# Decays of the cached keys, from a stage of their own into the score steps of an attention kernel

## The chip, the cores and the metric

The program runs on one core of one Trainium2 chip. The metric is the device time of one execution in microseconds (us).

## What is computed

Two layers of a decoder are run for a prompt of 2048 rows and for a group of 8 samples of one new row each. The change lies in the second layer, forgetting attention with 16 heads of 64. A sample attends to 4096 cached keys (32 pages of 128 rows) and to its new row:

```
csum = cumsum(concat([past_logf, logf]))           # along the keys
s = q.k * ATTN_SCALE + cq[..., :, None] - ck[:, :, None, :]
p = softmax(where(mask, s, -inf));  out = p @ v_all
```

The decay of a cached key is thus the sum of the log-forget values of all keys behind it. It depends on `cache_logf`, the page table and the new row alone, and has the shape of one number for each sample, head and key.

## The kernel before

The program is a row of stages. Each stage has its own semaphores and ends in a barrier of all engines. Behind the projections of layer 1 (`project1`) come `past`, `attention` and `out1`.

`past` makes the decays, in two groups (NG = 2) of 4 samples x 32 pages = 128 pages, one page on a partition. SyncE loads the page numbers, GpSimd gathers the log-forget rows of the pages with two indirect DMAs (1 MB each), VectorE runs 16 scans per group, one per head, TensorE adds up the totals of later pages with a matmul, VectorE turns the sums round (two passes over 128x2048), and TensorE transposes 32 blocks of 128x128, which VectorE copies into `C.decay`.

`attention` handles the prompt in 640 score steps: 16 heads x 4 chunks of 512 queries x 4, 8, 12 or 16 blocks of 128 keys. The order of everything on every engine is a list, `SEQ`, that `schedule()` writes out; each engine walks through it in order. A step `QK` has two or three matmuls on TensorE, an exp on ScalarE and an add into `acc` on GpSimd (weights go through a ring of 8). With each step goes one `M`, a matmul whose row maxima serve a chunk up to 22 steps ahead: VectorE reads it with a `reduce_max`. `M`, `MR` and `LS` share two PSUM banks, so that `M` number k waits until VectorE has read number k-2. `PV` weighs the values of four blocks; it comes behind the steps n with n mod 4 = 1. `OF` (VectorE) finishes a chunk.

The decode of the 8 samples is laid between these steps, as work at the end of given steps. For a sample: `SD` (VectorE adds decay to the scores), `SM` (maximum), `SA` (TensorE turns it, and waits for `SM`), `SB`, `SC`, `SS`, `SE` (exp), `SL` (sums), `SX` (TensorE, waits for `SL`), `SR`; then `VG` 0 to 7 (TensorE, 4 pages of values each, through the two halves of the tile `vp`), `VN` (the new row), `VM` (VectorE masks the result, `at_cm`), `VA` (TensorE, one-column matmuls, waits for `VM`) and `VC`. Before, a sample takes 80 steps, from step 0 on.

## Time and profile before

| | us |
|---|---|
| median of 3 runs | 3209.83 (3197.79 to 3213.23) |
| the profiled execution, its own time | 3206.77 |
| span of the profile | 3205.2 |
| TensorE busy | 2845.1 (89%) |
| VectorE, ScalarE, GpSimd busy | 1596.3, 1024.8, 1380.8 |

Times in the profile are counted from the span's start. `past` and `attention` lie between about 1894 and 2960 us. "PE" is the matmul, "PEld" the weight load of TensorE, DVE is VectorE, ACT ScalarE, POOL GpSimd, SP SyncE. What stands behind "<-" in a line of a wait is who ended it.

### The profile page before, as it was taken

The numbers are of one execution on the slowest core, as the hardware profiler recorded it, in microseconds if no ns is written. First come the engines' busy times: TensorE is split into PE (matmuls) and PEld (weight loads), VectorE is DVE, ScalarE is ACT, GpSimd is POOL, SyncE is SP. The second block draws the span as 40 slices with busy tenths as digits, with TensorE's granted clock in tenths as the row PEclk, the third lists the DMA queues.
The fourth block names the chain that finished last, engine by engine and source line by source line (L and its number), as shares of the span: only waits on it lengthen the run. The fifth ranks groups of instructions, "written<-read, shape, count | busy, mean of one in ns | idle before, by whom it ended". The sixth has DMA issues, their size and how long they took to land. (4 is left out here: it accounts for less than half of the span.)

```text
span 3205.2 us, 46929 instructions
## 1 busy us (share of the span) xinstructions
PE 2845.1 (89%) x17133; PEld 2257.1 (70%) x17133; DVE 1596.3 (50%) x2148; ACT 1024.8 (32%) x1721; POOL 1380.8 (43%) x986
## 2 busy tenths in 40 slices
PE   3887979695998999879999957999999999999999
PEld 2887878683674999879999954555555555554787
DVE  4222223234365579888555545455455555553432
ACT  4323232322245222212112212444444444544100
POOL 0000000001000477666988845766766777777000
PEclk9998989897999999989999986999999999999899
DMA  4101010104563688879777748877977877874532
GB/s 122 35 21 40 20 40 20 40 13 148 173 181 121 195 265 287 259 248 314 250 250 247 256 147 191 248 202 204 245 204 221 237 206 234 228 213 133 179 118 74
DMA packets 327904, 547.51 MB, mean 171 GB/s; under 512 B 76093, under 2 KB 220129, under 8 KB 319212
## 3 DMA queue, kind: packets, MB, share of 16 engines
q1 hardware_dynamic: 263564, 471.12, 49.9%
q10 hardware_dynamic: 61120, 58.83, 5.3%
q0 software_dynamic: 3008, 14.81, 1.3%
q8 instruction: 124, 2.03, 0.3%
q14 instruction: 88, 0.72, 0.1%
HBM read 449.58 MB, written 95.12 MB: 170 GB/s over the span
## 5 line engine op out<-in xcount | busy, mean ns | idle before, releaser
L1151 POOL TENSOR_TENSOR p_kp<-p_kp,p_qb 128x1024 f32<-128x1024 f32 x256 | 628.6, 2483 | 385.1 <-DMA p_kp<-in_cache_k_dram 305.3
L1993 POOL TENSOR_TENSOR at_acc<-at_acc,at_w 128x512 f32<-128x512 f32 (+3 forms) x576 | 644.0, 1118 | 250.8 <-ACT at_w L2121 186.2
L2153 DVE TENSOR_REDUCE at_mx<-at_mx 128x1 f32<-128x512 f32 (+3 forms) x640 | 382.8, 608 | 447.3 <-PE at_mx L2028 322.3
L112 PE MATMUL p_pb<-p_w,x_xh 128*128 128x256 f32 x2048 | 593.5, 290 | 8.1 <-DVE p_w L1465 8.0
L113 PE MATMUL p_pb<-p_w,x_xh 128*128 128x256 f32 x2048 | 580.8, 284 | 0.0
L114 PE MATMUL p_pb<-p_w,x_xl 128*128 128x256 f32 x2048 | 580.5, 283 | 0.0
L2121 ACT ACTIVATE at_w<-at_st,c_nckt 128x512 f32<-128x512 f32 (+3 forms) x640 | 390.0, 622 | 382.6 <-PE at_st L2054 195.8
L1567 DVE TENSOR_REDUCE p_sc<-p_kp 128x16 f32<-128x1024 f32 x256 | 307.5, 1214 | 219.9 <-POOL p_kp L1151 219.8
L112 PEld LDWEIGHTS p_pb<-p_w,x_xh 128*128 128x128 f32 x2048 | 392.4, 192 | 20.0 <-issue 11.0
L113 PEld LDWEIGHTS p_pb<-p_w,x_xh 128*128 128x128 f32 x2048 | 393.9, 192 | 0.0
L114 PEld LDWEIGHTS p_pb<-p_w,x_xl 128*128 128x128 f32 x2048 | 393.0, 192 | 0.0
L112 PE MATMUL l_pb<-x_xh,l_wh 128*128 128x412 f32 x800 | 289.1, 361 | 73.4 <-DVE l_wl L857 73.4
L2069 PE MATMUL at_o<-at_w,at_v 128*64 128x512 f32 (+3 forms) x1280 | 292.8, 558 | 0.5 <-ACT at_w L2121 0.5
L113 PE MATMUL l_pb<-x_xl,l_wh 128*128 128x412 f32 x800 | 286.2, 358 | 0.0
L114 PE MATMUL l_pb<-x_xh,l_wl 128*128 128x412 f32 x800 | 285.7, 357 | 0.0
L2028 PE MATMUL at_mx<-at_km,at_q 65*128 65x512 f32 (+3 forms) x640 | 254.0, 400 | 17.4 <-POOL at_onesh L1968 12.1
L2052 PE MATMUL at_st<-at_q,at_k 128*128 128x512 f32 (+3 forms) x640 | 268.1, 419 | 0.8 <-ACT at_w L2121 0.8
L112 PE MATMUL o_pp<-o_wh,o_mh 128*128 128x512 f32 (+1 forms) x544 | 220.7, 406 | 35.0 <-DVE o_wl L586 22.4
L2054 PE MATMUL at_st<-at_q,at_k 65*128 65x512 f32 (+3 forms) x640 | 238.8, 373 | 0.0
L2052 PEld LDWEIGHTS at_st<-at_q,at_k 128*128 128x128 f32 x640 | 122.6, 192 | 137.7 <-issue 113.4
L113 PE MATMUL o_pp<-o_wl,o_mh 128*128 128x512 f32 (+1 forms) x544 | 215.9, 397 | 0.0
L114 PE MATMUL o_pp<-o_wh,o_ml 128*128 128x512 f32 (+1 forms) x544 | 215.4, 396 | 0.0
(293 smaller groups left out, 3840.4 us busy)
## 6 DMA issues: line engine op xcount, KB each, us to landing
p_kp<-in_cache_k_dram SPq DMA_DIRECT2D x256, 512.0 KB, 4.9
at_vp<-in_cache_v_dram SPq DMA_DIRECT2D x256, 512.0 KB, 5.4
o_mt<-mixed SPq DMA_DIRECT2D x32, 512.0 KB, 5.4
p_raw<-in_w_in_dram SPq DMA_DIRECT2D x32, 512.0 KB, 7.2
at_q<-qh SPq DMA_DIRECT2D x32, 512.0 KB, 10.8
at_k<-kh SPq DMA_DIRECT2D x32, 512.0 KB, 8.5
l_raw<-in_w_in_dram SPq DMA_DIRECT2D x20, 512.0 KB
mixed<-l_w POOLq DMA_DIRECT2D x8, 1028.0 KB, 4.2
```

The costliest lines, as they stand in the source:

```text
L112: nc.tensor.matmul(out, lhs[0], rhs[0], start=(k == 0), stop=False)
L113: nc.tensor.matmul(out, lhs[0], rhs[1], start=False, stop=False)
L114: return nc.tensor.matmul(out, lhs[1], rhs[0], start=False, stop=(k == nk - 1))
L1151: nc.gpsimd.tensor_tensor(kp[:, g % 4], kp[:, g % 4], qb[:], ALU.mult).then_inc(kmul, 1)
L1567: nc.vector.tensor_reduce(sc[:, b % 2].rearrange("p (h g) -> p h g", g=z.PG)[:, :, r], by_head(kp[:, g % 4], z.H), AX.X, ALU.add).then_inc ...
L1993: nc.gpsimd.tensor_tensor(t[:, 512 - wd:512], t[:, 512 - wd:512], W[n % RW][:, 0:wd], ALU.add).then_inc(accd, 1)
L2028: last = nc.tensor.matmul(MX[r % 2][:, 0:wd], Q2[s][0:HR, t * P:(t + 1) * P], KM[s][0:HR, seg * 512:seg * 512 + wd], start=True, stop=seg < c)
L2052: nc.tensor.matmul(ST[n % 2][:, 0:wd], K1[s][:, ks], Q1[s][:, q0:q0 + wd], start=True, stop=False)
L2054: last = nc.tensor.matmul(ST[n % 2][:, 0:wd], K2[s][:, ks], Q2[s][:, q0:q0 + wd], start=False, stop=not diagonal)
L2069: last = nc.tensor.matmul(O[u % 2][y:y + HD, 512 - wd:512], V[s][:, kb + x, :], W[(n + x) % RW][:, 0:wd], start=kb + x < 2, stop=kb + x >= ...
L2121: nc.scalar.activation(W[n % RW][:, 0:wd], ST[n % 2][:, 0:wd], ACT.Exp, bias=C.nckt[:, kb, u // NC:u // NC + 1]).then_inc(ex, 1)
L2153: nc.vector.reduce_max(mx[:, u % 2, j, seg:seg + 1], MX[r % 2][:, 0:wd], AX.X).then_inc(mread, 1)
```

## The change

`past` is gone as a stage. Its work is laid into `SEQ`: the scans four at a time (`PS`, behind steps 16, 19, ... 37), the totals (`PT`, `PL`, `PA`, up to step 42), the turning round as one pass (`PM`, steps 43 to 50), the transposes (`PP`, steps 45 to 52, four each), the copies (`PC`, steps 47 to 54) and the new row (`PN`, 54). Its two large tiles lie in `vp`, so the first pages of values are loaded from step 54 on and not at the start. The decode's sample b begins at step 62 + 72 b, and takes 72 steps instead of 80. On GpSimd the setup is put in another order; the eight `affine_select` of `headmask` become `HM` behind steps 34, 38, ... 62. Page numbers are loaded behind the first three of the eight loads of head 0, and the gathers are issued then.

```diff
-        at = [1 + x for x in range(len(tail) - VG - 4)] + [13 + 8 * r for r in range(VG)] + [71, 72, 74, 76]
-        span = N // B
+        at = [x for x in range(len(tail) - VG - 4)] + [11 + 8 * r for r in range(VG)] + [68, 69, 70, 71]
+        span, first = 72, 62
         side = {}
+        for n in range(NG):
+            for x in range(H // 4):
+                m = H // 4 * n + x
+                side.setdefault(16 + 3 * m, []).append(("PS", n, x))
+                side.setdefault(43 + m, []).append(("PM", n, x))
+                side.setdefault(45 + m, []).append(("PP", n, x))
+                side.setdefault(47 + m, []).append(("PC", n, x))
+            side.setdefault(17 + 3 * (H // 4) * (n + 1), []).append(("PT", n))
+            side.setdefault(42, []).append(("PL", n))
...
+        for x in range(8):
+            side.setdefault(34 + 4 * x, []).append(("HM", x))
         for b in range(B):
             for w, x in zip(tail, at):
-                side.setdefault(span * b + x, []).append((*w, b))
+                side.setdefault(first + span * b + x, []).append((*w, b))
...
-            for x in range(NLD):
+            for x in range(3):
                 head_load(0, x)
+            for n in range(NG):
+                sp.dma_start(idx[:, n:n + 1], a["page_table"][n * z.SB:(n + 1) * z.SB, :].rearrange("b g -> (b g)")
+                             .rearrange("(q o) -> q o", o=1)).then_inc(idx_in, 16)
+            for x in range(3, NLD):
+                head_load(0, x)
...
+                elif w[0] == "PP":
+                    _, n, x = w
+                    m = H // 4 * n + x
+                    pe.wait_ge(dv, m + 1)
+                    if m >= 2:
+                        pe.wait_ge(copied, m - 1)
+                    else:
+                        pe.wait_ge(tadd, NG)
+                    for g in range(4):
+                        last = nc.tensor.transpose(CV[:, m % 2, g * GP:(g + 1) * GP], cum[n][:, 4 * x + g, :], C.ident[0:GP, 0:GP])
+                    last.then_inc(turned, 1)
...
+                elif w[0] == "PS":
+                    _, n, x = w
+                    if x == 0:
+                        dve.wait_ge(pmade, 1)
+                        dve.wait_ge(logf_in, 16 * NG)
+                    lv = logf[n].rearrange("q (t h) -> q t h", h=H)
+                    for h in range(4 * x, 4 * x + 4):
+                        last = nc.vector.tensor_tensor_scan(cum[n][:, h, :], onesp[:], lv[:, :, h], 0.0, ALU.mult, ALU.add)
+                    last.then_inc(scand, 1)
...
+                elif w[0] == "PM":
+                    _, n, x = w
+                    dve.wait_ge(tadd, n + 1)
+                    dve.wait_ge(totd, NG)
+                    nc.vector.scalar_tensor_tensor(out=cum[n][:, 4 * x:4 * x + 4, :], in0=cum[n][:, 4 * x:4 * x + 4, :], scalar=-1.0,
+                                                   in1=tot[:, n, 4 * x:4 * x + 4].rearrange("q (h o) -> q h o", o=1).broadcast_to([GP, 4, P]),
+                                                   op0=ALU.mult, op1=ALU.add).then_inc(dv, 1)
+                elif w[0] == "PC":
+                    _, n, x = w
+                    m = H // 4 * n + x
+                    dve.wait_ge(turned, m + 1)
+                    nc.vector.tensor_copy(C.decay[:, n * z.SB:(n + 1) * z.SB, 4 * x:4 * x + 4, 0:PG].rearrange("p b h g -> p h b g"),
+                                          CV[:, m % 2, 0:4 * GP].rearrange("p (h b g) -> p h b g", h=4, g=PG)).then_inc(copied, 1)
```

Where it moves instructions, VectorE first, at steps 16 to 31, before. `at_mx` rows are reads of `M`, `at_og` rows are `OF`.

```order
L2153 TENSOR_REDUCE at_mx<-at_mx 128x1 x7
L2168 TENSOR_TENSOR at_og<-at_o,at_ot 64x512
L2171 TENSOR_TENSOR at_og<-at_og,at_sg 64x512
L2153 TENSOR_REDUCE at_mx<-at_mx 128x1
L2159 TENSOR_REDUCE at_mneg<-at_mx 128x4
L2153 TENSOR_REDUCE at_mx<-at_mx 128x1 x12
L2159 TENSOR_REDUCE at_mneg<-at_mx 128x4
```

And now; the rows with `at_onesp` are the scans of `PS` (the listing calls a scan SCALAR_TENSOR_TENSOR, and the tiles inside `vp` by that name).

```order
L2144 TENSOR_TENSOR at_og<-at_o,at_ot 64x512
L2147 TENSOR_TENSOR at_og<-at_og,at_sg 64x512
L2129 TENSOR_REDUCE at_mx<-at_mx 128x1
L2135 TENSOR_REDUCE at_mneg<-at_mx 128x4
L2129 TENSOR_REDUCE at_mx<-at_mx 128x1 x2
L2155 SCALAR_TENSOR_TENSOR at_vp<-at_onesp,at_vp 128x128 x4
L2129 TENSOR_REDUCE at_mx<-at_mx 128x1 x2
L2135 TENSOR_REDUCE at_mneg<-at_mx 128x4
L2129 TENSOR_REDUCE at_mx<-at_mx 128x1
L2155 SCALAR_TENSOR_TENSOR at_vp<-at_onesp,at_vp 128x128 x4
L2129 TENSOR_REDUCE at_mx<-at_mx 128x1 x3
L2155 SCALAR_TENSOR_TENSOR at_vp<-at_onesp,at_vp 128x128 x4
```

Four scans now stand behind every third read. Next TensorE, where the first sample's decode ends, before: the one-column matmuls of `VA` at the end of step 74.

```order
L2069 MATMUL at_o<-at_w,at_v 64x512 x4
L2052 MATMUL at_st<-at_q_1,at_k_1 128x512
L2054 MATMUL at_st<-at_q_1,at_k_1 128x512
L2028 MATMUL at_mx<-at_km,at_q_0 128x512
L2108 MATMUL at_cv<-c_onescol,at_cm 128x1 x8
L2052 MATMUL at_st<-at_q_1,at_k_1 128x512
```

And now, steps 130 to 132 (`VN`, then `VM` on VectorE behind step 131, then `VA` behind step 132).

```order
L2076 MATMUL at_cv<-at_vp,at_sw 32x512 x2
L2008 MATMUL at_st<-at_q_1,at_k_1 128x128
L2010 MATMUL at_st<-at_q_1,at_k_1 128x128
L2012 MATMUL at_st<-at_identr,at_maskr 128x128
L1983 MATMUL at_mx<-at_km,at_q_1 128x512
L2008 MATMUL at_st<-at_q_1,at_k_1 128x512
L2010 MATMUL at_st<-at_q_1,at_k_1 128x512
L1983 MATMUL at_mx<-at_km,at_q_1 128x512
L2083 MATMUL at_cv<-c_onescol,at_cm 128x1 x8
```

The `PV` (`at_o`) that stood between `VM` and `VA` is not there any more. Last, TensorE at steps 46 to 48 now, with the transposes of `PP` (`at_cv<-c_ident,at_vp`); before, none of them stood in this stage.

```order
L2050 MATMUL at_cv<-c_ident,at_vp 128x128 x4
L2008 MATMUL at_st<-at_q_1,at_k_1 128x512
L2010 MATMUL at_st<-at_q_1,at_k_1 128x512
L1983 MATMUL at_mx<-at_km,at_q_1 128x512
L2050 MATMUL at_cv<-c_ident,at_vp 128x128 x4
L2008 MATMUL at_st<-at_q_1,at_k_1 128x512
L2010 MATMUL at_st<-at_q_1,at_k_1 128x512
L2012 MATMUL at_st<-at_identr,at_maskr 128x128
```

Each group of four follows a single score step, and waits for a copy that VectorE makes behind its read of that step's `M`.

## Rows read from the trace of the kernel before

**Rows 1.** The profile's page: busy time, share of the span, instructions.
```profile
PE 2845.1 (89%) x17133; PEld 2257.1 (70%) x17133; DVE 1596.3 (50%) x2148; ACT 1024.8 (32%) x1721; POOL 1380.8 (43%) x986
```
**Rows 2.** Seven windows of 80 steps: us; PE, PEld, DVE, ACT, POOL busy; clock; DMA.
```profile
2351.30:2480.30 129.00, 125.86 (x666) 71.80 (x665) 67.42 (x118) 60.10 (x100) 88.69 (x82) 0.95 0.79 214
...
2727.70:2850.50 122.80, 119.64 (x666) 68.82 (x665) 67.28 (x118) 60.10 (x100) 88.98 (x82) 1.00 0.79 224
sum 877.86, PE 856.18 PEld 491.13 DVE 471.76 ACT 420.68 POOL 620.87; mean PE 122.31 PEld 70.16 DVE 67.39 ACT 60.10 POOL 88.69
```
**Rows 3.** Timelines of SP, DVE, PE around `past`: start, duration, what, idle before.
```profile
1894.55 0.83 SPq L1592 DMA_DIRECT2D pa_idx<-in_page_table_dram  x2
1932.55 0.50 SPq L1857 DMA_DIRECT2D at_q<-qh  x1
...
1906.15 5.15 DVE L1639 TENSOR_TENSOR_SCAN pa_cum<-pa_ones,pa_l 128x128 f32<-128x128 f32 x16 [26.59 <-DMA pa_l<-in_cache_logf_dram,pa_idx]
1924.83 1.28 DVE L1657 COPY c_decay<-pa_pt 128x512 f32<-128x512 f32 x2
...
1942.77 0.47 PE L2028 MATMUL at_mx<-at_km,at_q 65*128 65x128 f32 x1 [12.10 <-POOL at_onesh L1968]
1954.69 0.77 PE L2052 MATMUL at_st<-at_q,at_k 128*128 128x512 f32 x1
```
**Rows 4.** Tile `at_k`, window 1930 to 1960: the last load of head 0.
```profile
L1857 SPq DMA_DIRECT2D at_k<-kl x1: 623/623/623, 1936.7 to 1936.7; - x1
...
DMA to landing us min/median/max: 8.8/10.7/16.0
```
**Rows 5.** Windows: head 0's loads; then the gathers of `past`.
```profile
1934.00:1950.00 16.00, 5.73 (x18) 3.89 (x18) 4.81 (x11) 0.58 (x1) 15.25 (x19) 0.50 1.02 219
1899.50:1905.50 6.00, 0.00 (x0) 0.00 (x0) 0.00 (x0) 0.00 (x0) 0.10 (x1) 0.50 0.82 330
```
**Rows 6.** Timelines of PE and PEld: two `M`, `PV` and the next `M`, transposes, `VA`.
```profile
2012.17 0.40 PE L2028 MATMUL at_mx<-at_km,at_q 65*128 65x512 f32 x1
...
2012.87 0.39 PE L2028 MATMUL at_mx<-at_km,at_q 65*128 65x512 f32 x1
...
2203.13 1.94 PE L2069 MATMUL at_o<-at_w,at_v 128*64 128x512 f32 x8
...
2205.57 0.40 PE L2028 MATMUL at_mx<-at_km,at_q 65*128 65x512 f32 x1
...
1880.00 0.46 PEld L1241 LDWEIGHTS p_tp<-c_ident,p_rows 128*128 128x128 f32 x4
...
2205.57 1.99 PEld L2108 LDWEIGHTS at_cv<-c_onescol,at_cm 128*128 128x128 f32 x16
```
**Rows 7.** Timeline of DVE: the read of the `M` issued at 2205.57.
```profile
2206.00 0.69 DVE L2153 TENSOR_REDUCE at_mx<-at_mx 128x1 f32<-128x512 f32 x1 [1.44 <-PE at_mx L2028]
```
**Rows 8.** Waits, 1972 to 2960: who waited for whom, us, times, longest.
```profile
PEld at_cv L2087 <- DVE at_l L2196: 10.3, 7, 1.5
PEld at_cv L2081 <- DVE at_smx L2182: 8.0, 7, 1.2
```
**Rows 9.** Groups of DVE, 1972.64 to 2960: busy us, mean ns, idle before.
```profile
L2205 DVE SCALAR_TENSOR_TENSOR at_cm<-at_cv,at_rl,at_headmask 128x1024 f32<-128x1024 f32 x8 | 10.2, 1276 | 7.5 <-PE at_cv L2101 7.5
...
L2178 DVE TENSOR_TENSOR at_sd<-at_sc,c_decay 128x512 f32<-128x512 f32 x7 | 8.5, 1210 | 0.0
```
**Rows 10.** Timelines of DVE and POOL at two places where both read SBUF.
```profile
1991.10 0.95 DVE L2171 TENSOR_TENSOR at_og<-at_og,at_sg 64x512 f32<-64x512 f32 x1
1991.65 1.54 POOL L1993 TENSOR_TENSOR at_acc<-at_acc,at_w 128x512 f32<-128x512 f32 x1
...
1960.04 0.71 DVE L2179 TENSOR_TENSOR at_sd<-at_sn,c_decay 128x16 f32<-128x16 f32 x1
1959.83 0.88 POOL L1993 TENSOR_TENSOR at_acc<-at_acc,at_w 128x256 f32<-128x256 f32 x1 [0.26 <-ACT at_w L2121]
```
**Rows 11.** Line L2179 (ns min/median/max), and L1993 by form (busy us, mean ns).
```profile
L2179 DVE TENSOR_TENSOR at_sd<-at_sn,c_decay x8: 175/179/712, 1960.0 to 2843.6; 128x16 f32<-128x16 f32 x8
...
L1993 POOL TENSOR_TENSOR at_acc<-at_acc,at_w 128x512 f32<-128x512 f32 x383 | 502.6, 1312 | 186.8 <-ACT at_w L2121 143.8 <-POOL at_acc L1993 1.3 <-POOL at_acc L1990 0.4
```

More of the change, by code:

```diff
@@ L1680, in attention @@
     VG = PG // 4
+    NG = B // z.SB
+    GP = z.GP
+    assert GP == P and NG * H * P * 2 <= 8 * z.D
     RW = 8
@@ L1812, in attention @@
         vp = S.sb("vp", [P, 2, 4, z.D])
+        flat = vp[:].rearrange("p s g d -> p (s g d)")
+        logf = [flat[:, P * H * n:P * H * (n + 1)] for n in range(NG)]
+        cum = [flat[:, P * H * (NG + n):P * H * (NG + n + 1)].rearrange("q (h t) -> q h t", t=P) for n in range(NG)]
+        idx = S.sb("idx", [GP, NG], I32)
+        onesp = S.sb("onesp", [GP, P])
+        tot = S.sb("tot", [GP, NG, H])
+        beyond = S.sb("beyond", [GP, GP])
+        lnew = S.sb("lnew", [1, B * H])
         sc = S.sb("sc", [P, H * PG])
@@ L1922, in _ @@
                     scores(w[-1] + 1)
+                elif w[0] == "PN":
+                    sp.wait_ge(turned, NG * H // 4)
+                    value_group(0, 0)
+                    value_group(0, 1)
                 elif w[0] == "VG":
@@ L1952, in _ @@
         def _(pool):
-            for s in range(2):
-                nc.gpsimd.memset(K2[s][HD:HR].bitcast(F32), 1.0).then_inc(made, 1)
-                nc.gpsimd.memset(Q2[s][HD:HR].bitcast(F32), 1.0).then_inc(onesd, 1)
+            nc.gpsimd.memset(maskf[:], 0.0).then_inc(masked, 1)
+            pool.wait_ge(masked, 1)
+            nc.gpsimd.affine_select(out=maskf[:], in_=maskf[:], compare_op=ALU.is_ge, fill=NEG, base=0,
+                                    pattern=[[-1, P]], channel_multiplier=1).then_inc(masked, 1)
+            nc.gpsimd.memset(onesp[:], 1.0).then_inc(pmade, 1)
+            nc.gpsimd.memset(beyond[:], 1.0).then_inc(pmade, 1)
+            nc.gpsimd.memset(C.decay[:, :, :, PG:PX], NEG).then_inc(pmade, 1)
+            pool.wait_ge(pmade, 3)
+            nc.gpsimd.affine_select(out=beyond[:], in_=beyond[:], compare_op=ALU.is_gt, fill=0.0, base=0,
+                                    pattern=[[-1, GP]], channel_multiplier=1).then_inc(pmade, 1)
+            pool.wait_ge(pmade, 4)
+            lv = beyond[:].rearrange("q (b g) -> q b g", g=PG)
+            nc.gpsimd.affine_select(out=lv, in_=lv, compare_op=ALU.is_ge, fill=0.0, base=PG - 1,
+                                    pattern=[[PG, z.SB], [0, PG]], channel_multiplier=-1).then_inc(pmade, 1)
+            pool.wait_ge(pmade, 5)
+            nc.gpsimd.memset(Q2[0][HD:HR].bitcast(F32), 1.0).then_inc(onesd, 1)
+            nc.gpsimd.memset(K2[0][HD:HR].bitcast(F32), 1.0).then_inc(made, 1)
+            pool.wait_ge(made, 1)
+            pool.wait_ge(onesd, 1)
+            pool.wait_ge(idx_in, 16 * NG)
+            for n in range(NG):
+                pool.indirect_dma_start(out=logf[n], out_offset=None, in_=a["cache_logf"].rearrange("n p h -> n (p h)"),
+                                        in_offset=bass.IndirectOffsetOnAxis(ap=idx[:, n:n + 1].bitcast(U32), axis=0)).then_inc(logf_in, 16)
+            nc.gpsimd.memset(Q2[1][HD:HR].bitcast(F32), 1.0).then_inc(onesd, 1)
+            nc.gpsimd.memset(K2[1][HD:HR].bitcast(F32), 1.0).then_inc(made, 1)
             pool.wait_ge(made, 2)
@@ L2074, in _ @@
                     pe.wait_ge(accd, HB * (h + 1))
+                    pe.wait_ge(made, 3)
                     ring_free(r)
@@ L2445, in hybrid_step @@
             C.decay = S.sb("decay", [P, z.B, z.H, z.PX])
-            past(nc, z, a, C, out)
             attention(nc, z, a, C, D, out)
```

149 lines of the change are left out of this document (44 added, 105 removed).

## The prediction

> **What bounds the kernel now.** First the page: TensorE is busy 89% of the span, no other engine above half [rows 1]. Then windows over the attention stage: of 122.80 us that a sample's 80 steps take at best, TensorE is busy 119.64, GpSimd 88.98, VectorE 67.28 [rows 2]. So in this stage the order on TensorE is the time. A microsecond of TensorE's work or waiting is a microsecond of the kernel; work of VectorE is free as long as TensorE does not come to wait for it. The same windows show a second thing. The seven sum to 877.86 us, which is 18.3 more than 7 x 122.80, and the longest (129.00) has a mean granted clock of 0.95, against 1.00 in the best [rows 2]: the low level (1.2 GHz instead of 2.4) costs 1 to 6 us a sample. Third the timelines around `past`. Its first DMA is issued at 1894.55, attention's first at 1932.55, TensorE does nearly nothing between; attention's first matmul is at 1942.77 and its first score step at 1954.69 [rows 3].
>
> **The change, part by part.**
>
> The stage goes: 1932.55 - 1894.55 = **-38.0** [rows 3]. The logf gather's latency (VectorE stood 26.59 us before its first scan) lies in these 38.
>
> The start of attention gets the gathers. Before, the first score step came 22.1 us after the first issue. The last load of head 0 was issued at 1936.7 and landed 16.0 later, at 1952.7, so 20.2 after the first [rows 4]; the loads ran at 219 GB/s with the DMA engines full (share 1.02) [rows 5]. The two gathers (2.1 MB) took some 6 us at share 0.82 in an empty machine [rows 5], so 4.9 us of all engines. They now fall between those loads and push the last landing to about 25.1, and with its semaphore the first score step to some 25.6: **+3.5**. Bounds: -2 (loads untouched, 20.2), +6.
>
> TensorE gets 32 transposes and two pairs of small matmuls. Four transposes at the full clock took 0.43 (1880.00 to the next load; the row has 0.46) [rows 6], eight groups 3.6, the matmuls some 0.7: **+4.3**. Bounds 3 and 7 (low clock).
>
> `PP` waits. From the issue of an `M` (2205.57) to the read of it (2206.00) pass 0.43 us [rows 6, 7]; the read takes 0.6 net of overlap (0.69 in its row), the copy `PC` 0.6 (two in 1.28) [rows 3], the semaphore 0.1: 1.7 to 1.8. TensorE has 0.23 of that filled (two `M` of neighbouring steps with both score matmuls between are 0.70 apart, three matmuls of 0.23) [rows 6]. `PP` number m waits for the copy m-2 behind the read of its own step, so it waits 1.5 us wherever no `PV` lies between: steps 47, 48, 50, 51, 52. **+7.5**. Queued behind it: the next score step, so ScalarE and GpSimd too. Bounds 2 and 10.
>
> `PS`. Alone a scan is 0.32 (16 in 5.15) [rows 3], four are 1.3. With three reads of 0.6 VectorE would need 3.1 us in three steps. TensorE takes 4 x 0.70 for four steps and 1.9 for their `PV` (2203.13 to the next `M` at 2205.57, less that step's own 0.5) [rows 6], so 3.5 for three: hidden. But not beside GpSimd. A multiply with two inputs in SBUF took 0.95 as GpSimd was adding, and GpSimd's next add 1.54 [rows 10] against a mean of 1.31 [rows 11]; a tiny operation with both inputs in SBUF, of 0.18 as a rule, took 0.71 and ended with the add beside it (1960.76 and 1960.71) [rows 10, 11]. The scans have both inputs in SBUF, GpSimd's adds of 512 columns take 1.3 each [rows 11], and one comes with each step, in stretches where steps without `PV` are 0.70 apart [rows 6]. So each scan can meet an add. If none does: 0. If each of the four waits a whole add: 3.1 + 4 x 1.3 = 8.3 us for three steps instead of 3.5, x8 = +38. I take half the adds met, 5.6 for 3.5, x8 = 17, less 2 for the groups in narrow steps: **+15**. The two banks that `M` shares carry the delay to TensorE.
>
> The Trainium skill (SBUF — State Buffer, Who interferes with whom) says that a VectorE instruction with two SBUF inputs and a GpSimd instruction that reads SBUF lock each other out for a whole instruction. That speaks for the upper end, where each scan waits out an add; the trace's 0.71 for 0.18 agrees with it, and only shows it for one operation at a time.
>
> The decode's new positions modulo 4. A `PV` (n mod 4 = 1) gives VectorE 1.9 us to catch up. `SA` waited 8.0 us in 7 samples, `SX` 10.3 in 7 [rows 8], `VA` never. Now `SD` (1.21 mean [rows 9], plus 0.18) stands behind a step without `PV`, and `SM` and `SA` behind the next two: 0.43 + 0.6 + 1.4 + 0.6 + 0.7 from the `M` of the first = 3.75, of which TensorE fills 1.6; the wait goes from 1.15 to 2.2, +1.1 x 8 = 9. `SX` gets a `PV` between it and `SL`: -10 x 8/7, about -11, but in three samples an `OF` (1.6) falls before `SL`, +4. `VM` takes 1.28 [rows 9] and `VA` follows one step later with no `PV` between: 0.43 + 0.6 + 1.28 + 0.1 - 0.9 = 1.5, x8 = 12. Net **+14**. Bounds 0 and 22. Queued behind `VA` are all score steps.
>
> The clock. `VA` is 16 weight loads with one-column matmuls, 1.99 us [rows 6], in which the array does next to nothing; the 18.3 us lost to the low level [rows 2] lie right behind it. Now it has 1.5 us of standing still ahead of it, and 2.2 more four steps later. I take the low level behind each of the eight at 3.7 us: 30 - 18 = **+12**. Bounds 0 and 22.
>
> Small: VectorE is freed of the first sample's decode while two `M` a step are read, -2; the low clock in the `PP` steps, +3. Setup on GpSimd, `HM` (8 x 1.04, the ring of 8 weights hides it), the tail (last `VC` behind step 637 instead of 636), the value pages (first used at step 73, loaded from 54): 0. Were the cover of `HM` gone it would cost 8.
>
> Sum: -38.0 + 3.5 + 4.3 + 7.5 + 15 + 14 + 12 + 1 = +19.3, on the profiled execution's own 3206.77: 3226. That execution lies 3.1 under the median, the measured runs spread by 15. **3227.**
>
> **Rivals.**
>
> (a) The cover holds; **3189**. The stage's 38 us come back nearly whole: scans meet few adds, the clock behaves as before. -38 + 3.5 + 4.3 + 5 + 3 + 4 + 0 = -18. For it: VectorE is busy only 67.28 of 122.80 us [rows 2]. Against it: the waits in rows 8, which stand there at 55% busy.
>
> (b) Halves cancel; **3210**. The waits of `PS` and of the positions come out at half. -38 + 3.5 + 4.3 + 6 + 8 + 10 + 7 = +1. For it: the bounds of three terms begin at 0.
>
> (c) The lock decides; **3248**. Each scan waits for a whole add, +38 instead of +15. It is slower than (the forecast) from about 2 us a scan on. For it rows 10; against it, that GpSimd runs out of adds when TensorE is held up.
>
> That the stage's work is not removed but only overlaps is sure from the order; the pages of values arriving late (72 steps instead of 80) I give next to nothing: pages still come 8 steps apart and 16 ahead, and the busiest windows have a DMA share of 0.79 [rows 2].
>
> **How the numbers follow.** Forecast (slower by some 0.5 to 0.9%) 0.42, (c) 0.10, (b) 0.30, (a) 0.18. A measurement of this kernel tells about 0.5% (16 us) from no change. The forecast's own range is 3218 to 3240; since it begins at the edge of 0.5%, a part of it (0.07) counts as no change. Slower 0.45, same 0.36, faster 0.19. For 8 in 10 the range takes in (b), most of (a) and most of (c): 3184 to 3246.
>
> **What would show it.** In the profile after: the first score step 25 to 26 us after attention's first DMA issue (right: start). Scans with a median above 0.6 us and TensorE waiting for VectorE's reads of `at_mx` by 10 us or more between steps 16 and 40 (right: `PS`; with scans near 0.4, (a)). TensorE waiting on `c_decay`'s copies about 1.5 us, five times. Waits on `at_cm` of 1.5 us, eight times, and on `at_smx` of 2.2; those on `at_l` mostly gone. Granted clock 0.93 to 0.96 over the samples' windows of 72 steps, with a low stretch behind each `VA`. The prediction is wrong if the scans slip between the adds, or if the clock stays high past `VA`; then it is (a) or (b).

## The result, and the profile after

The changed kernel took 3261.15 us (median of 4 runs, 3258.00 to 3266.26) against 3204.07 for the one before (3197.79 to 3213.23): ratio 1.0179, 95% interval 1.0153 to 1.0205, so +57 us. It is slower, as forecast, but by three times as much as the forecast's +19, and outside the range. In all that follows a ratio is that to the kernel before, run beside it on the same chip; 0.001 is 3.2 us.

Windows from the first exp of step 0 to that of step 80 and of step 639, so heads 0 and 1 and then the other fourteen (columns as in [rows 2]). First the kernel before:

```profile
1956.98:2090.93 133.95, 131.09 (x661) 76.44 (x661) 70.08 (x126) 59.45 (x97) 86.83 (x81) 0.90 0.87 236
2090.93:2958.02 867.09, 844.54 (x4611) 481.55 (x4610) 459.22 (x803) 419.08 (x690) 619.43 (x572) 0.98 0.76 213
```

The same windows after:

```profile
1916.80:2080.23 163.43, 135.13 (x567) 80.17 (x567) 108.72 (x177) 59.92 (x97) 95.66 (x88) 0.82 0.46 110
2080.23:3010.74 930.51, 889.39 (x4743) 495.31 (x4742) 467.83 (x805) 420.98 (x690) 624.66 (x573) 0.96 0.77 215
```

The score steps begin 40.2 us earlier (1916.80 for 1956.98), so the stage is gone as planned. Then they take 1093.9 us instead of 1001.0: +92.9. Of these, 29.5 lie in the first two heads, where the decays' work is and hardly any decode, and 63.4 in the other fourteen, where nothing of the decays is left. The two parts are not like for like: the kernel before has a whole sample's decode in its first two heads, and after all eight samples fall on the other fourteen (4743 matmuls there for 4611). The clock says how. With levels of 1.2 and 2.4 GHz, a mean clock c of full speed means that a share 2(1 - c) of the time ran at the low one: 163.4 x 0.36 + 930.5 x 0.08 = 133 us after, 134.0 x 0.20 + 867.1 x 0.04 = 61 before. TensorE spent some 70 us more at half speed (rounding leaves 20 on this), and each costs half a microsecond at most: about 35. The two traces' records of the clock, added up without rounding, have 137.8 us at the low level after (59.3 in the first two heads) and 53.7 before (26.4): 84 more, so the cost is at most 42.

The rest is waiting. The waits of TensorE's matmuls in the 640 steps (who for whom, us, times, longest), before:

```profile
PE at_mx L2038 <- DVE at_mx L2153: 10.2, 32, 0.9
PE at_cv L2081 <- DVE at_smx L2182: 5.9, 7, 0.9
PE at_mx L2028 <- DVE at_mx L2153: 4.1, 8, 0.6
PE at_cv L2087 <- DVE at_l L2196: 4.1, 7, 0.6
```

And after (TensorE's line numbers are 45 to 25 lower than before; L1983 is `M`, L2055 `SA`, L2062 `SX`, L2050 `PP`, L2083 `VA`):

```profile
PE at_mx L1983 <- DVE at_mx L2129: 18.8, 8, 4.6
PE at_cv L2055 <- DVE at_smx L2195: 14.9, 6, 3.3
...
PE at_cv L2062 <- DVE at_l L2209: 9.2, 7, 2.7
PE at_cv L2050 <- DVE c_decay L2177: 7.7, 5, 1.8
PE at_cv L2083 <- DVE at_cm L2218: 6.6, 8, 1.3
```

That is +14.7 at `M`, +9.0 at `SA`, +5.1 at `SX`, +7.7 at `PP`, +6.6 at `VA`: 43. With 6 for the added transposes (the busy time of their row) and up to 42 for the clock it makes up to 91 of the 93. TensorE's busy time says the same without the clock. It is the sum of the two windows of each kernel, before and after:

```profile
sum 1001.04, PE 975.63 PEld 557.99 DVE 529.30 ACT 478.53 POOL 706.25; mean PE 487.81 PEld 278.99 DVE 264.65 ACT 239.26 POOL 353.13
sum 1093.94, PE 1024.52 PEld 575.48 DVE 576.55 ACT 480.90 POOL 720.32; mean PE 512.26 PEld 287.74 DVE 288.27 ACT 240.45 POOL 360.16
```

TensorE stands still for 69.4 us instead of 25.4 (+44.0), and its work takes 1024.5 instead of 975.6 (+48.9), though only 38 more matmuls are counted. Waits of its weight loads are counted too further on; they begin earlier and so are longer (at `SA` 17.7 us for the matmuls' 14.9, at `SX` 11.8 for 9.2, at `VA` 9.2 for 6.6).

Where a wait and the clock meet is best seen at a sample's change-over. Timelines of TensorE, VectorE and GpSimd after, steps 131 to 137:

```profile
2161.46 0.39 PE L1983 MATMUL at_mx<-at_km,at_q 65*128 65x512 f32 x1
2163.13 2.96 PE L2083 MATMUL at_cv<-c_onescol,at_cm 128*128 128x1 f32 x16 [1.28 <-DVE at_cm L2218]
...
2167.52 2.82 PE L2025 MATMUL at_o<-at_w,at_v 128*64 128x512 f32 x8
...
2176.22 0.38 PE L2055 MATMUL at_cv<-c_ident,at_smx 128*16 128x128 f32 x1 [3.31 <-DVE at_smx L2195]
...
2172.04 1.75 DVE L2191 TENSOR_TENSOR at_sd<-at_sc,c_decay 128x512 f32<-128x512 f32 x1
2173.72 1.24 DVE L2192 TENSOR_TENSOR at_sd<-at_sn,c_decay 128x16 f32<-128x16 f32 x1
...
2171.97 4.35 POOL L1941 TENSOR_TENSOR at_acc<-at_acc,at_w 128x512 f32<-128x512 f32 x3 [2.74 <-ACT at_w L2096]
```

TensorE stands 1.28 us for `VM`, runs `VA` in 2.96 us (its weight loads in 2.88, for 1.99 in [rows 6]) and the `PV` behind it in 2.82 (1.94 in [rows 6]). Two steps on `SD` takes 1.75 + 1.24 us, beside three adds of GpSimd (experiment 13 tests that they are the reason), and `SA` is waited for 3.31 us; the score matmul behind that took 0.77 us where that of the step before took 0.51. Windows of the same stretch: the wait for `VM`, the first microsecond of `VA`, the rest of it with the `PV`, the steps up to `SA`'s wait, that wait, and what follows it (the last three columns are clock, DMA share and GB/s):

```profile
2161.85:2163.13 1.28, 0.00 (x0) 0.00 (x0) 1.28 (x3) 0.50 (x1) 0.61 (x1) 1.00 1.06 282
2163.13:2164.13 1.00, 1.00 (x8) 1.00 (x8) 0.55 (x1) 0.00 (x0) 0.00 (x0) 0.85 0.97 238
2164.13:2170.27 6.14, 6.14 (x22) 4.17 (x22) 0.64 (x2) 0.69 (x1) 1.26 (x1) 0.50 0.97 346
2170.27:2172.90 2.63, 2.63 (x10) 1.72 (x9) 1.46 (x2) 2.15 (x4) 0.93 (x1) 0.93 1.03 412
2172.90:2176.20 3.30, 0.01 (x1) 0.00 (x0) 3.30 (x5) 0.51 (x1) 3.01 (x3) 0.68 1.27 249
2176.20:2180.70 4.50, 4.48 (x13) 1.94 (x13) 3.24 (x7) 0.69 (x1) 1.39 (x2) 0.50 1.05 222
```

The clock is high over the wait for `VM`, falls inside `VA`, comes back, and falls again during the wait for `SA`. In the whole trace it falls within 4 us of the start of seven of the eight `VA` (before: four of eight), and a second time some 10 to 15 us behind the start of six of them. Windows of steps 120 to 128, 128 to 152 and 152 to 160 show that the loss is in this place alone (clock 1.00, 0.86, 1.00):

```profile
2140.56:2153.16 12.60, 12.29 (x75) 7.09 (x75) 6.51 (x12) 7.02 (x13) 8.68 (x10) 1.00 0.57 151
2153.16:2202.75 49.59, 44.26 (x210) 25.35 (x210) 27.06 (x47) 18.85 (x30) 26.62 (x25) 0.86 0.67 192
2202.75:2214.27 11.52, 11.52 (x63) 6.17 (x63) 4.52 (x8) 4.75 (x8) 9.48 (x9) 1.00 0.75 217
```

In the first head the scans do the same. VectorE, GpSimd and TensorE after, from step 15 on:

```profile
1944.34 5.63 DVE L2155 TENSOR_TENSOR_SCAN at_vp<-at_onesp,at_vp 128x128 f32<-128x128 f32 x4
...
1942.75 8.35 POOL L1941 TENSOR_TENSOR at_acc<-at_acc,at_w 128x512 f32<-128x512 f32 x6 [1.04 <-ACT at_w L2096]
...
1952.30 0.58 PE L1983 MATMUL at_mx<-at_km,at_q 65*128 65x256 f32 x1 [4.60 <-DVE at_mx L2129]
```

Four scans and the adds beside them take turns: 5.63 / 4 = 1.41 us a scan, 8.35 / 6 = 1.39 us an add. TensorE then stands 4.60 us. The next four scans took 1.36 us: TensorE had been held up, and GpSimd had no add until 1955.61. The eight groups took 5.63, 1.36, 1.90, 2.43, 5.54, 1.36, 5.33 and 1.36 us.

### The profile page after: what moved, and what is told of

Its sections match the earlier page's. It is cut to its first block and busy times, and to the rows that moved or that the text cites. A ratio compares the mean times of both kernels' runs of the same rounds, so it can differ in the third digit from the quotient of the medians.

```text
span 3258.8 us, 46976 instructions
## 1 busy us (share of the span) xinstructions
PE 2881.9 (88%) x17133; PEld 2262.4 (69%) x17133; DVE 1618.3 (50%) x2152; ACT 1027.2 (32%) x1721; POOL 1387.4 (43%) x986
## 5 line engine op out<-in xcount | busy, mean ns | idle before, releaser
L2025 PE MATMUL at_o<-at_w,at_v 128*64 128x512 f32 (+3 forms) x1280 | 314.1, 593 | 0.5 <-ACT at_w L2096 0.5
L1983 PE MATMUL at_mx<-at_km,at_q 65*128 65x512 f32 (+3 forms) x640 | 255.7, 402 | 33.4 <-DVE at_mx L2129 19.5
L2008 PE MATMUL at_st<-at_q,at_k 128*128 128x512 f32 (+3 forms) x640 | 275.8, 431 | 3.2 <-issue 2.4
```

What stands on the lines that cost most here:

```text
L1983: last = nc.tensor.matmul(MX[r % 2][:, 0:wd], Q2[s][0:HR, t * P:(t + 1) * P], KM[s][0:HR, seg * 512:seg * 512 + wd], start=True, stop=seg < c)
L2008: nc.tensor.matmul(ST[n % 2][:, 0:wd], K1[s][:, ks], Q1[s][:, q0:q0 + wd], start=True, stop=False)
L2025: last = nc.tensor.matmul(O[u % 2][y:y + HD, 512 - wd:512], V[s][:, kb + x, :], W[(n + x) % RW][:, 0:wd], start=kb + x < 2, stop=kb + x >= ...
```

## Experiments

Two theories stood against each other: A, the decode's new places are most of the loss; B, the work of the decays among the score steps is. The edits are to the changed kernel unless the text says otherwise, and the diffs show the lines that matter. The interval of a ratio is 0.002 to 0.004 to each side, so a difference between two experiments is known to some 9 to 16 us; where it is smaller than that, the traces have to carry the argument.

**1. The decode alone.** In the kernel before, with its stage:

```diff
-        at = [1 + x for x in range(len(tail) - VG - 4)] + [13 + 8 * r for r in range(VG)] + [71, 72, 74, 76]
-        span = N // B
+        at = [x for x in range(len(tail) - VG - 4)] + [11 + 8 * r for r in range(VG)] + [68, 69, 70, 71]
+        span, first = 72, 62
```

> The kernel before, its stage `past` kept, with only the decode's steps changed to those of the changed kernel (begin at 62, 72 a sample, same offsets). Theory A: the decode's new places are most of the loss. In the trace of after, heads 2 to 15, which hold nothing of the decays, take 930.5 us against 867.1 before, +63; so this kernel should be +50 to +65 us on before (3254 to 3269), with waits on at_smx and at_cm and a low stretch of the clock behind nearly each VA. Theory B: the work of the decays in steps 16 to 55 is most of it, and what heads 2 to 15 lose follows from it (a late start, a shifted GpSimd); then this one is +10 to +25 (3214 to 3229).

3259.48 us, ratio 1.0176 (1.0136 to 1.0216). The whole +57 is here, to within 15 us. Theory A holds, and the decays' work in the score steps costs about what the stage gave back, some 38 us. Its profiled execution was its slowest (3281.77 us; the others 3258.01 to 3264.40). Heads 0 and 1 in it, with neither decays nor a decode, and the rest:

```profile
1969.19:2090.96 121.77, 116.38 (x529) 71.51 (x529) 72.15 (x124) 59.48 (x97) 86.29 (x80) 0.89 0.55 131
2090.96:3031.35 940.39, 894.19 (x4743) 497.02 (x4742) 468.08 (x805) 420.94 (x690) 624.85 (x574) 0.95 0.77 213
```

Against this the decays' work made the first two heads 41.7 us longer (163.43), more than the 29.5 against the kernel before. Over all 640 steps the difference is 31.8 us (1093.94 for 1062.16), where the changed kernel's steps begin 40.2 us earlier than those of before. TensorE's matmuls wait in experiment 1 as they do after: 14.8 us at `SA`, 9.2 at `SX`, 6.6 at `VA`. Experiments 2 to 4 ran beside it.

**2. The chain spaced out.**

```diff
-        at = [x for x in range(len(tail) - VG - 4)] + [11 + 8 * r for r in range(VG)] + [68, 69, 70, 71]
+        at = [0, 0, 2, 2, 4, 4, 5, 6, 8, 8] + [11 + 8 * r for r in range(VG)] + [67, 68, 70, 71]
```

> The changed kernel with the chain of the decode's steps spaced: SD and SM at 0, SA and SB at 2, SC and SS at 4, SE 5, SL 6, SX and SR 8, VN 67, VM 68, VA 70, VC 71. Each piece of VectorE now has a PV or a second step between it and TensorE's next piece. Theory A (TensorE's waits at SA, SX and VA, and the low clock that follows a wait): waits on at_smx, at_l, at_cm fall from 17.7 + 11.8 + 9.2 us to under 10 together, the low stretches behind VA from about 17 to under 8, time -40 to -60 on after (3200 to 3220). Rival: the low clock follows the 16 one-column matmuls of VA itself, wait or not; then only the waits go, -20 to -30 (3231 to 3241), and the low stretches stay.

3249.34 us, ratio 1.0143 (1.0103 to 1.0184): -12, less than either forecast. The waits at `SX` went, those at `VA` fell to 2.2 us (matmuls), but those at `M` rose from 18.8 to 24.9, and those at `SA` stayed (12.3 us, five times, up to 2.8): `SD` and `SM` both stood at step 134 and `SA` two steps on, before the next `PV`.

**3. The scans' ones from PSUM.**

```diff
+                        nc.vector.tensor_copy(CV[0:GP, 1, 0:P], onesp[:]).then_inc(cvones, 1)
-                        last = nc.vector.tensor_tensor_scan(cum[n][:, h, :], onesp[:], lv[:, :, h], 0.0, ALU.mult, ALU.add)
+                        last = nc.vector.tensor_tensor_scan(cum[n][:, h, :], CV[0:GP, 1, 0:P], lv[:, :, h], 0.0, ALU.mult, ALU.add)
```

> The changed kernel with the ones that each scan multiplies by read from PSUM (the decode's buffer, free until step 42) instead of SBUF, so that a scan has one input in SBUF. Theory (the scans and GpSimd's adds hold each other up because both of a scan's inputs lie in SBUF): the scans' time, 393/415/1500 ns minimum, median, longest, loses its long ones (longest under 700), the two groups of four of 5.6 us fall to about 1.7, the waits of TensorE for the reads of at_mx in steps 16 to 40 shrink by some 8 us, and the time by 8 to 15 us with the clock (3246 to 3253). Rival (VectorE is late because of what it has to do, and a PSUM input is no faster): scans stay as they are or get slower, and the time stays within 4 us of after.

3240.36 us, ratio 1.0115 (1.0076 to 1.0155): -21, more than expected. The scan's line (ns min/median/max) after, and here:

```profile
L2155 DVE TENSOR_TENSOR_SCAN at_vp<-at_onesp,at_vp x32: 393/415/1500, 1944.3 to 1995.3; 128x128 f32<-128x128 f32 x32
```

```profile
L2158 DVE TENSOR_TENSOR_SCAN at_vp<-at_cv,at_vp x32: 390/397/424, 1950.1 to 1981.0; 128x128 f32<-128x128 f32 x32
```

With one input in SBUF no scan is held up, while GpSimd's adds go on. TensorE's waits at `M` in the first two heads fell from 16.3 to 3.4 us and these heads took 145.2 us for 163.4; the other fourteen took 930.5 in both.

**4. The decays' pieces behind a PV.** Scans at 9 + 4m, transposes in pairs behind a `PV`:

```diff
-                side.setdefault(16 + 3 * m, []).append(("PS", n, x))
-                side.setdefault(45 + m, []).append(("PP", n, x))
-                side.setdefault(47 + m, []).append(("PC", n, x))
+                side.setdefault(9 + 4 * m, []).append(("PS", n, x))
+                side.setdefault(45 + 4 * (m // 2), []).append(("PP", n, x))
+                side.setdefault(46 + 4 * (m // 2) + m % 2, []).append(("PC", n, x))
...
```

`PM` moves with them (42 + 2m), as do the totals and `PN`.

> The changed kernel with the pieces of the decays moved to steps whose number modulo 4 is 1, where TensorE has a PV: scans at 9 + 4m, transposes in pairs at 45, 49, 53, 57, their copies one and two steps later. Decode as in after. Theory (the decays' pieces cost where they stand, in steps without a PV): waits on the copies of c_decay (7.7 + 11.2 us) fall to under 3, waits on at_mx in the first two heads from 38 us to under 20, the low stretches in steps 16 to 62 from 5 to at most 2; heads 0 and 1 take 140 us or less instead of 163.4, the time -20 to -28 (3233 to 3241). Rival (it is the amount of VectorE's and TensorE's work in a head that is already late from its start, wherever it stands): heads 0 and 1 stay above 155, the time above 3250.

3255.56 us, ratio 1.0156 (1.0114 to 1.0199): -7 by the ratio, no difference that can be told from none; by its time it is the rival's, by its first two heads (148.2 us for 163.4) between the two. The waits on `c_decay` are gone; but the scans met more adds than after (median 0.644 us for 0.415), and the other fourteen heads took 6 us more in this trace (936.6).

**5. VA two steps behind VM, with a PV between.**

```diff
-... + [68, 69, 70, 71]
+... + [69, 70, 72, 73]
```

> The changed kernel with the last four steps of a sample at 69, 70, 72, 73 instead of 68, 69, 70, 71: VA comes two steps and a PV behind VM, at a step that is 2 modulo 4, as before. SD to SX stay. Theory (TensorE stands 1.2 us for VM, then runs VA and the PV behind it at 1.2 GHz): the waits on at_cm vanish, the first of the two low stretches of a sample (at 133, 205, 277, ...) goes, a sample's change-over gets 4 to 6 us shorter, time -28 to -40 (3221 to 3233). Rival (the low clock comes from VA's one-column matmuls, or from SA's wait): only the 9 us of waits go, 3248 to 3254.

3237.16 us, ratio 1.0109 (1.0074 to 1.0144): -22, between the two forecasts. The waits at `VA` (9.2 us of weight loads, 8 times) are gone, and steps 128 to 152 take 42.50 us for 49.59, at a clock of 0.92:

```profile
2152.28:2194.78 42.50, 41.58 (x210) 23.61 (x210) 26.20 (x47) 18.84 (x30) 26.51 (x25) 0.92 0.81 224
```

Here is the surprise: the waits at `SA` (weight loads) fell too, from 17.7 us to 5.1, though `SD`, `SM` and `SA` did not move. `VA` now stands between steps 134 and 135, so that the exps of these steps come 2.5 us apart (2163.83 and 2166.33) and the adds with them (in this trace from 2164.60 and from 2167.09, where after three stood in a row); `SD`'s second addition met none (median 0.176 us, after 1.240).

**6. SD as copies (the decays left out of the scores).**

```diff
-                    nc.vector.tensor_tensor(sd[:, :, 0:PG], sc[:]..., C.decay[:, b, :, 0:PG], ALU.add).then_inc(sdd, 1)
+                    nc.vector.tensor_copy(sd[:, :, 0:PG], sc[:]...).then_inc(sdd, 1)
```

> The changed kernel with both additions of SD made copies of the scores: the decays are left out of the scores, so that each of the two reads one input from SBUF instead of two; same places, same sizes. Theory (SD and GpSimd's adds hold each other up, which is why SA is waited for up to 3.7 us): SD's two operations fall from 1.75 + 1.24 us to about 0.7 + 0.1, the waits on at_smx from 17.7 to under 6 us, the second low stretch of a sample goes, time -15 to -35 (3226 to 3246). Rival (SA waits since two reads of at_mx and SD follow each other in three steps of 0.70 us, whatever SD takes): waits on at_smx stay above 10 us, time above 3250.

3256.51 us, ratio 1.0160 (1.0123 to 1.0196): -6, nothing to speak of. But it did not test what it should. The copy of 16 columns here (ns min/median/max):

```profile
L2192 DVE COPY at_sd<-at_sn x8: 428/1235/1236, 2054.1 to 2900.1; 128x16 f32<-128x16 f32 x8
```

It was held up as long as the addition with two inputs (median 1.240 us), and the waits at `SA` hardly fell (13.5 us for 14.9, matmuls). My premise, that one input in SBUF is enough to be free, fell. The Trainium skill (VectorE: DVE Perf Modes, Mode 2×_2P) says that a copy from SBUF to SBUF streams its one input through both read ports; this agrees with 1.235 us for 16 columns.

**7. All decode steps at their old places modulo 4.**

```diff
+        at = [x - 1 for x in range(len(tail) - VG - 4)] + [11, 19, 27, 35, 43, 51, 59, 63] + [65, 66, 68, 70]
```

> The changed kernel with every decode step at the place modulo 4 that it had before (SD 1, SM 2, SA 3, ..., VN 3, VM 0, VA 2, VC 0), with the same distances between VG7, VN, VM, VA, VC as before; for room the last group of pages comes 4 steps behind the one before it instead of 8. Samples still come every 72 steps. Theory A1 (the places modulo 4, so the missing PV, make the loss): the 13 low stretches behind step 120 fall to 5 or fewer, the change-overs cost 3 to 4 us instead of 10 to 13, time -45 to -60 (3200 to 3216). Theory A2 (72 steps walk the chain through the phases of a head of 40 steps, 80 steps kept SD and VA in the same place, SD beside GpSimd's short adds on narrow steps): VA's waits go, but SD keeps its 1.7 + 1.0 us in most samples and SA its waits, time -15 to -35 (3226 to 3246).

3227.23 us, ratio 1.0075 (1.0046 to 1.0103): -33, at the edge of the forecast of theory A2 and short of A1's. `VA` waits no more, `SA` 11.2 us for 17.7 (weight loads). The edit also puts the last group of pages four steps behind the one before it.

**8. Experiments 3, 4 and 7 together.**

> e3 (the ones of the scans in PSUM), e4 (decays' pieces where a PV is) and e7 (the old places modulo 4) together. If the three act on separate places, their differences add up: -21 of e3, -6 of e4 less what both share, and e7's. With A1 the time is 3180 to 3195, below the kernel before (3204); with A2 3200 to 3225. Rival: what one takes away another was hiding, and the sum is less than two thirds of the single differences.

3199.65 us, ratio 0.9992 (0.9974 to 1.0011), so -60 (some 10 to either side): the single differences (-21, -7, -33) add up. That is what separate causes, the decays and the decode, would give.

**9 and 10. Phase or closeness.** Both in the kernel before: 9 has the `at` of experiment 7 with `span, first = 72, 2`; 10 has

```diff
-... + [13 + 8 * r for r in range(VG)] + [71, 72, 74, 76]
+... + [17 + 8 * r for r in range(VG)] + [75, 76, 78, 79]
```

> The kernel before with its stage kept and the decode as in e7 (old places modulo 4, VG7 four steps after VG6, 72 steps a sample), but begun at step 2, so that SD stands at steps 1, 73, 145, 217, 289, 361, 433, 505: the phases 1, 33, 25, 17, 9, 1, 33, 25 of a head's 40 steps. Before, it stood at phase 1 in all. Theory A2 (the phase in the head counts): the change-over of the sample at step 361 (phase 1) costs about as much as those of before, 4 us over 60.3 a head and little low clock, the others 8; time about 3225. Theory A3 (the last steps of a sample and the first of the next now stand next to each other, 132 and 133, where before 76 and 81): the one at 361 costs 8 like the others. Theory A4: neither, all cost 4, and e7's excess came from the decays in the first heads; time about 3204.

> The kernel before with the pages and the last four steps of each sample 4 steps later (VG at 17 + 8r, VN 75, VM 76, VA 78, VC 79), so that VC stands two steps before the next SD instead of five; places modulo 4 and 80 steps kept (VC's alone 3 for 0). Theory A3 (closeness): each of the seven change-overs costs 3 to 5 us more, time +20 to +35 (3225 to 3240). Theory A2 (phase): VA at phase 38 of a head for 34, SD at 1 as before: within 8 us of before.

9: 3219.05 us, ratio 1.0040 (1.0018 to 1.0063). 10: 3212.86, ratio 1.0028 (1.0003 to 1.0052). So of the 57 us of experiment 1 some 44 go once the places modulo 4 are right and the decode begins early; in the kernel before no run parts the two. The change-over at step 361, in the old phase, was no cheap one (steps 340 to 380: 66.51 us at 0.97, the 40 behind them 60.16 at 1.00): phase is not it. Closeness costs 9 us in experiment 10 (1 to 17 by its interval), less than A3 asked for. What the other few us of 9 are stays open.

**11. Experiments 3, 4 and 5 together.**

> e3, e4 and e5 together: the decays as in e8, the decode with only its last four steps at 69, 70, 72, 73. Single differences to the changed kernel: e3 -21, e4 -6, e5 -24. If they add up, 3210; e8, which has all of the decode at its old places, took 3199.7 with -61. If the difference of e7 to e5 (10 us) lies in the first two heads, where e7 has 158 us and e5 163, this one is 3205 to 3212.

3196.67 us, ratio 0.9981 (0.9956 to 1.0005): -63, for a sum of -50, which the noise allows. With a sample's last four pieces moved the kernel is as good as with all of its chain moved as well (experiment 8); the two intervals overlap.

**12. VA in two halves**, on experiment 8:

```diff
-            + [("VG", r) for r in range(VG)] + [("VN",), ("VM",), ("VA",), ("VC",)]
+            + [("VG", r) for r in range(VG)] + [("VN",), ("VM",), ("VA", 0), ("VA", 1), ("VC",)]
...
+        at = [x - 1 for x in range(len(tail) - VG - 5)] + [11, 19, 27, 35, 43, 51, 59, 63] + [65, 66, 68, 69, 70]
...
-                    for k in range(z.KB):
+                    for k in range(z.KB // 2 * w[1], z.KB // 2 * (w[1] + 1)):
```

> e8 with VA in two halves, eight of its sixteen one-column products at step 68 and eight at 69 of a sample. Theory C (the 2 us in which the array does nearly nothing let the clock fall, wait or no wait): of e8's ten low stretches behind a change-over most go, each change-over gets 2 to 4 us shorter, time 3175 to 3190, below the kernel before. Rival (the low clock is due to the waits for VectorE at SA and SX, 9.8 and 7.7 us in e8): low stretches and time stay as in e8, 3196 to 3204.

3192.35 us, ratio 0.9961 (0.9941 to 0.9981): some 10 us below experiment 8 (9 to either side), and below the kernel before. The effect is between the two forecasts. In the last fourteen heads of experiment 8's trace and of this one the time was 900.8 and 887.7 us, in the first two, which this edit does not touch, 131.5 and 138.6; so far apart can two traces lie without a cause in the kernel.

**13. SD reads PSUM** (the cached scores left out, sizes kept):

```diff
-                    nc.vector.tensor_tensor(sd[:, :, 0:PG], sc[:]..., C.decay[:, b, :, 0:PG], ALU.add).then_inc(sdd, 1)
+                    nc.vector.tensor_tensor(sd[:, :, 0:PG], CV[:, 0, 0:H * PG]..., C.decay[:, b, :, 0:PG], ALU.add).then_inc(sdd, 1)
```

> The changed kernel with both additions of SD reading the decode's PSUM buffer in place of the cached scores: the cached scores are left out, each addition keeps its size and has one input in SBUF (the decays) and one in PSUM. Theory L (SD is slow because GpSimd's adds hold it up; e6's copies, which lay wholly in SBUF, were held up as well: 1.26 and 1.00 us): now SD takes about 0.7 + 0.1 us in every sample, the waits on at_smx fall from 17.7 to under 6 us, the change-overs get 2 to 3 us shorter, time -15 to -25 on after (3236 to 3246). Rival (SD's length does not matter, SA waits for the reads in front of it): SD gets short and the waits stay above 12 us, time within 6 us of after.

3248.10 us, ratio 1.0133 (1.0101 to 1.0164): -15; one of its five runs took 4125.90 us and is not in the ratio. The small addition here:

```profile
L2192 DVE TENSOR_TENSOR at_sd<-at_cv,c_decay x8: 176/177/179, 2043.1 to 2869.5; 128x16 f32<-128x16 f32 x8
```

0.18 us in all eight samples, the large one 0.68, and the waits at `SA` from 17.3 to 8.1 us (weight loads, heads 2 to 15). Theory L holds, if not to the full (it had asked for under 6 us of waits), and repairs the failed test of experiment 6: half of `SA`'s wait is `SD` held up by adds, and the other half stays when `SD` is short.

**14. Only SD to SR one step earlier.**

```diff
+        at = [x - 1 for x in range(len(tail) - VG - 4)] + [11 + 8 * r for r in range(VG)] + [68, 69, 70, 71]
```

> The changed kernel with only the ten steps SD to SR one step earlier (SD at a step that is 1 modulo 4 and holds a PV, as before); pages, VN, VM, VA, VC stay. Together with e5, which moved only the last four, it splits what e7 moved at once. My prediction priced SA's and SX's new places at +9 and -7 us. If the two parts add up to e7, this one is -10 (3251). If VA's wait is what delays VectorE and GpSimd for SD (e5: SD's second addition fell from 1.01 to 0.18 us although SD did not move), this one alone brings at most -10, and the waits on at_cm stay at 9 us; if SD's place matters by itself, the waits on at_smx fall below 9 us and the time by 15 or more (3246 or less).

3238.70 us, ratio 1.0090 (1.0058 to 1.0122): -29. `SD`'s place matters by itself. The waits at `SA` fell from 17.7 to 8.7 us, those at `VA` stayed at 9.2 (weight loads). With -22 (experiment 5) and -33 (both, experiment 7) the two do not seem to add up. The medians leave that open; in the traces the 640 steps got shorter by 37.6, 23.4 and 35.0 us in experiments 5 (its fastest run), 14 and 7. It fits that each breaks the same chain of wait, low clock and next wait.

**15. Each TensorE piece of the chain behind a PV of its own**, on experiment 12:

```diff
+        at = [-1, 0, 3, 3, 7, 7, 8, 9, 11, 11] + [15, 23, 31, 39, 47, 55, 59, 63] + [65, 66, 68, 69, 70]
```

> e12 with each of TensorE's pieces of the chain behind a PV of its own: SD -1, SM 0, SA and SB 3, SC and SS 7, SE 8, SL 9, SX and SR 11, pages at 15, 23, 31, 39, 47, 55, 59, 63. Theory (what a sample still costs in e12 are waits for VectorE at SA and SX, 7.6 and 8.4 us, and the low clock behind them): both waits go, at most three low stretches remain behind step 120, time -10 to -16 on e12 (3176 to 3182), 0.7% or more below the kernel before. Rival (two pairs of page groups 4 steps apart, or one-column products, now set it: the clock falls as before): within 4 us of e12.

3188.24 us, ratio 0.9929 (0.9903 to 0.9955): -10 against experiment 12, the least that was forecast and at the edge of the noise. The matmuls' waits at `SA` and `SX` are gone. A new one stands in their place, value pages that come late for the groups four steps apart:

```profile
PE at_cv L2076 <- DMA at_vp<-in_cache_v_dram: 9.3, 6, 2.4
```

**16. Pages seven steps apart**, on experiment 15: `[15, 22, 29, 36, 43, 50, 57, 63]`.

> e15 with its eight groups of pages 7 steps apart (15, 22, 29, ..., 57, 63) instead of 8 and twice 4. In e15 TensorE waits 16.2 us nine times for value pages that land late, at the groups that stand 4 steps behind the one before. Theory: those waits go, time -8 to -14 on e15 (3174 to 3180). Rival (they lay beside other waits, or the pages now collide with the loads of the heads): within 4 us of e15.

3175.72 us (3169.13 to 3179.11), ratio 0.9911 (0.9893 to 0.9930): -6 against experiment 15, not clear of the noise, for 8 to 14 forecast. The page waits fell to 0.5 us, once. Heads 0 and 1, then the rest:

```profile
1918.73:2043.10 124.37, 116.25 (x567) 72.88 (x567) 94.17 (x178) 59.43 (x98) 97.47 (x89) 0.95 0.57 131
2043.10:2920.43 877.33, 862.35 (x4743) 483.12 (x4742) 464.30 (x805) 420.25 (x690) 623.54 (x572) 0.99 0.83 230
```

The same count of TensorE's instructions as after, 92.2 us less: 124.37 for 163.43 and 877.33 for 930.51.

**17. The same two decode edits in the kernel before** (80 steps a sample, stage kept):

```diff
+        at = [1, 2, 5, 5, 9, 9, 10, 11, 13, 13] + [17, 25, 33, 41, 49, 57, 63, 69] + [71, 72, 74, 75, 76]
```

> The kernel before, stage kept, 80 steps a sample, with the same two edits of the decode as in e15: VA in two halves, each TensorE piece of the chain behind its own PV (SD 1, SM 2, SA and SB 5, SC and SS 9, SE 10, SL 11, SX and SR 13; pages 17 to 57 by 8, 63, 69). It tells what moving the decays is worth once the decode is placed well. Theory: the 18 us of waits at SA and SX and most of the seven low stretches go, -20 to -30 (3176 to 3186), so that the change brings nothing by itself, since its 38 us are spent on the decays' work among the score steps. Rival: before had little to lose there, this one stays above 3195 and e15's gain is the moved stage.

3192.54 us, ratio 0.9953 (0.9932 to 0.9974), on the chip of experiment 16. Mended in the same way, the kernel without the change gains 0.5%, some 15 us, between the two forecasts; the one with it is faster still, by 17 us in the medians and by 13 in the ratios (0.9911 / 0.9953 = 0.9958; 9 to either side). My theory that moving the decays brings nothing is wrong once their pieces are well placed: of its 38 us some 13 to 17 stay.

## Why the prediction was wrong

The reading of what bounds the kernel, and the direction, were right. (The sum's 19.3 and the 3.1 make 3229 and not 3227, and rival (c) 3252 and not 3248; nothing hangs on it.) By its own steps:

- **The stage gone, -38.0**: right (the first issue at 1893.33, attention at once).
- **The gathers, +3.5**: nothing came of it. The first score matmul was at 1915.46, 22.1 us after the first issue, as before; the gathers were issued at 1902.36 and 1903.71, behind all eight loads of head 0, the last of which was issued at 1898.30, and not between them.
- **`PP` waits, +7.5**: right, 7.7 us, five times.
- **`PS`, +15**: right in kind, and in size as far as can be told. Experiment 3 gives 21, known to 15, the clock behind the waits included; in its trace the waits fell by 12.9 us and the first two heads by 18.2. The sign that I had named was split: TensorE waited 16.3 us for the reads in the first two heads, but the scans' median was 0.415 us, near the 0.4 of rival (a). The 32 scans took 24.9 us together, but not half of the adds were met everywhere: three groups of four took 5.3 to 5.6 us, each scan with a whole add, and the group behind each of them 1.36. Rival (c)'s mechanism holds for three groups of eight, where scans and adds took turns (some 1.4 us a scan); what was said against it, that GpSimd runs out of adds when TensorE is held up, spares the next group.
- **The places modulo 4, +14**: `VA` +12 was 9.2 us of waits, eight times, longest 1.7. `SA` +9 was +9.3 (8.0 to 17.3, samples 1 to 7), but half of the 17.3 is `SD` held up by adds (experiment 13), which I had priced with its 1.21 us from [rows 9]: there it stood beside the head's narrow first steps. `SX` -11 + 4 was wrong. Its wait stayed: 10.3 became 8.7 in the samples of heads 2 to 15, and 11.8 with the first. `SL` takes 1.94 + 0.25 us and stands behind a read of 0.7, which a `PV` of 1.9 does not cover.
- **The clock, +12 (and +3)**: this is the step that failed. I took the low level behind each of the eight `VA` at 3.7 us and no more. The runs show a chain: wait, low level, a `PV` at half speed, a row of adds behind it, `SD` held up, the wait at `SA`, low level again. Steps 128 to 152 alone took 7.1 us less with `VA` moved (experiment 5). In all the low level cost up to 42 us, not 15: up to 26 in heads 2 to 15, where the sum had 12, and up to 16 in the first two, where it had 3. Of the 38 us by which the forecast fell short that is up to 27; the waits were 7 more than forecast, and the rest are small terms and the noise of the runs. Taking out `VA`'s wait gave back 22 us and moving `SD` to `SR` 29, where their own waits fell by 9 each; the rest is low level and the waits further down the chain (with `VA` moved, `SA`'s fell by 12.6 as well).

The sum of the waits was thus nearly right (8 + 15 + 14 forecast, 44 measured); the bound of 22 on the clock looked at `VA` alone and left out that every other new wait (`M`, `SA`, `SX`, `PP`) can lower it as well. Experiment 1 says the same by place: the decode cost 57, for which the sum had 14 + 12. What the runs leave open is how these 57 divide: the places modulo 4 account for 33 (experiment 7), and for the other 24 the late begin, the closeness of the samples (9 in experiment 10) and the one-column products of `VA` (10 in experiment 12) are candidates that were not told apart in this kernel.
